# Up projection: the gate's sigmoid from exponentials and a logarithm on ScalarE, the weight low parts on VectorE

## The chip, the core and the metric

The program runs on one core of one Trainium2 chip. The metric is the device time of one execution in microseconds (us), the median of a few runs. A core has five engines that each work through a queue of their own: TensorE (PE; its weight loads are listed as PEld), VectorE (DVE), ScalarE (ACT), GpSimd (POOL) and SyncE (SP, which here only starts transfers). They wait for one another through semaphores.

## The reference, cut to what matters

The whole program is two blocks of a network on a 1024 x 1024 activation. The change touches one matrix product of the second block and the activation behind it:

```python
D_FF = 2816
def conv_ffn(h, w_up, conv_w, conv_b, w_down):
    T = h.shape[1]                       # 1024 positions
    u = h @ w_up                         # (1024 x 1024) @ (1024 x 5632)
    up = jnp.pad(u, ((0, 0), (CONV_W - 1, 0), (0, 0)))
    c = conv_b + sum(up[:, j:j + T] * conv_w[j] for j in range(CONV_W))   # 3 taps
    gate, val = jnp.split(c, 2, axis=-1)
    return (jax.nn.gelu(gate) * val) @ w_down
```

`jax.nn.gelu` is the tanh form, which is the same as gate * sigmoid(s * gate * (1 + 0.044715 gate^2)) with s = 2 sqrt(2/pi).

## The kernel before, in words

Every matrix product is done in three passes on rounded parts: a weight block W is split into a high part (ScalarE copies it to the rounded type, line 3469 in this phase, 401 in the others) and a low part (W minus the high part, line 3474 in this phase, 406 in the others); the activations are split likewise. TensorE adds up high x high, high x low and low x high.

The phase around the change is `up_part`. Its 2816 hidden columns are worked off in 22 groups j of 128 gate columns and the 128 value columns that belong to them. Of each group TensorE computes two units, ("up", j, 0), the gate, and ("up", j, 1), the value, each [128 columns x 1024 positions] in PSUM, in two pieces of 512 positions with 24 matmuls each (line 3541). A group is 96 matmuls. The units go round four PSUM banks.

The order on each queue is written out by hand; no scheduler moves anything. For one group:

- SyncE loads the weights of group j (line 3483) once unit ("up", j-2, 1) is done, since groups j and j-2 have the same slot of W.
- ScalarE, in iteration j: the high part of group j+1 (`up_w_hi`), the centre tap of the gate (line 3584), its square (3588), the exponential (3590), the centre tap of the value (3584).
- GpSimd: the low part of each group from 1 to 21 (`up_w_lo`), one after another. That of group 0 is made on VectorE, in the phase before.
- VectorE, in iteration j: the two other taps of the gate (3601, 3603; the second frees the PSUM bank), then the argument of the sigmoid (3614, 3615), 1 + the exponential (3617), the reciprocal (3618), the product with the gate (3619), the two taps of the value (3601, 3603) and the product of both (3624), which is written into `act_turned`.
- TensorE: groups 0 and 1 begin before all rows of the activation are there. It first does the left piece of all four units of groups 0 and 1. Behind the first and the second of these pieces it turns the last two row blocks (line 625) that the phase before (`out2`) has left over; then it does the four right pieces, and from group 2 on group after group. Before the left pieces of group 1, and before each later group, it waits for that group's low part (`K.up_lo`).

The phase before ends on VectorE with lines 602 and 616: value and low part of the turned rows; the last row block can only be finished when TensorE has turned it. The phase behind is `down`, the product with w_down. Its first weight block is split early (in iteration 21). Its second is loaded into a slot of W that unit ("up", 21, 1) frees, and split by lines 401 (ScalarE) and 406 (VectorE), followed by the low part of the activation (2571 on ScalarE, 2622 on VectorE). TensorE needs all of this for the second step of `down`. The third block goes where the gate's buffer is, so SyncE waits for `s_cg`, which VectorE gives after the last gate product.

Of the kernel before, what the change touches and what calls it, by code (L numbers as in the profile page):

```python
# [29 lines left out]
ALU = mybir.AluOpType  # L30
ACT = mybir.ActivationFunctionType
# [3426 lines left out]
def up_slots(K):  # L3458

    return [(K.pl.items[("down", 0, 0)] + n) % 3 for n in range(3)]  # L3460


def up_half(K, j, hi, W):
    return W[:, up_slots(K)[j % 2], HALF * hi:HALF * hi + HALF]


def up_w_hi(K, a, j):
    a.wait_ge(K.up_in[j % 2], 32 * (j // 2 + 1))
    a.activation(up_half(K, j, 1, K.Wr), up_half(K, j, 0, K.W), ACT.Copy).then_inc(K.up_hi, 1)


def up_w_lo(K, eng, j):
    eng.wait_ge(K.up_hi, j + 1)
    eng.tensor_tensor(up_half(K, j, 0, K.Wr), up_half(K, j, 0, K.W), up_half(K, j, 1, K.Wr).bitcast(F32), ALU.subtract)\  # L3474
        .then_inc(K.up_lo, 1)


def load_up(K, sp, j, done):

    dst = K.W[:, up_slots(K)[j % 2], 0:HALF].rearrange("p (k n) -> p k n", n=2 * P)  # L3480
    for half in range(2):
        c0 = FF * half + P * j
        sp.dma_start(dst[:, :, P * half:P * half + P],
                     K.i["w_up_2"][0][:, c0:c0 + P].rearrange("(k p) n -> p k n", p=P)).then_inc(done, 16)


def up_part(K, st, rows):

    nc = K.nc
    NJ = FF // P
    K.AT = nc.alloc_sbuf_tensor_at("act_turned", [P, NJ, T], F32, offset=K.base + 4 * 6 * T)
    K.ATr = nc.alloc_sbuf_tensor_at("act_turned_rounded", [P, NJ, T], F32R, offset=K.base + 4 * 6 * T)

    CUBE, SLOPE = 0.044715, 2 * math.sqrt(2 / math.pi)
    HL = K.uHL  # L3500
    slots = up_slots(K)
    cg = K.W[:, slots[2], 0:HALF].rearrange("p (a t) -> p a t", a=2)
    cv = K.W[:, slots[2], HALF:2 * HALF].rearrange("p (a t) -> p a t", a=2)
    G = K.ps(st, "G", [P, 4, T])
    first = K.pl.units[("up", 0, 0)]
    s_cg = K.sem("up_last_gate")
    s_c, s_sq, s_arg, s_e, s_at = (K.sem("up_centre"), K.sem("up_square"), K.sem("up_gelu_arg"),
                                   K.sem("up_gelu_exp"), K.sem("up_act_ready"))

    def bank(key):  # L3510
        return G[:, (K.pl.units[key] - first) % 4, :]

    def ht(k):
        return K.HTr[:, k, 0:T].rearrange("p (s n) -> p s n", n=C)

    def ht_lo(k):
        if k < 6:
            return HL[:, k, :].rearrange("p (s n) -> p s n", n=C)
        return K.HTr[:, 4 * (k - 6):4 * (k - 6) + 4, T:R]

    def sync(sp):
        for j in range(2, NJ):
            K.wait_unit(sp, ("up", j - 2, 1))
            load_up(K, sp, j, K.up_in[j % 2])
        for j in (NJ - 2, NJ - 1):
            K.wait_unit(sp, ("up", j, 1))
            K.load_item(sp)
        sp.wait_ge(s_cg, 1)

    def gpsimd(g):  # L3530
        for j in range(1, NJ):
            up_w_lo(K, g, j)

    def tensor(pe):
        def piece(j, half, rc):
            w = [up_half(K, j, n, K.Wr).rearrange("p (k n) -> p k n", n=2 * P) for n in range(2)]
            c = slice(P * half, P * half + P)
            for k in range(KT):
                x = [ht_lo(k), ht(k)]
                for a, b in SPLIT_PASSES:  # L3540
                    ins = pe.matmul(bank(("up", j, half))[:, rc * 512:rc * 512 + 512], w[a][:, k, c],  # L3541
                                    x[b][:, 2 * rc:2 * rc + 2, :], start=(k == 0 and a == b == 1),
                                    stop=(k == KT - 1 and a == 0))
            return ins

        early = [(j, half) for j in range(2) for half in range(2)]
        for n, (j, half) in enumerate(early):
            if half == 0:
                pe.wait_ge(K.up_lo, j + 1)
            if n == 0:  # L3550
                rows.taken(pe, rows.late[0] - 1)
                rows.ready(pe, 4)
            elif n < 3:
                rows.taken(pe, rows.late[n - 1])
            else:
                rows.turns_read(pe)
            piece(j, half, 0)
            if n < 2:
                rows.turn(pe, rows.late[n])
        rows.ready(pe, 8)  # L3560
        for j, half in early:
            piece(j, half, 1).then_inc(K.gemm_done, 1)
        for j in range(2, NJ):
            pe.wait_ge(K.up_lo, j + 1)
            for half in range(2):
                K.wait_bank(pe, ("up", j, half), 4)
                piece(j, half, 0)
                piece(j, half, 1).then_inc(K.gemm_done, 1)

    def scalar(a):  # L3570
        rows.done(a)
        for j in range(NJ):
            if 1 <= j and j + 1 < NJ:
                up_w_hi(K, a, j + 1)
            if j == NJ - 1:
                K.split_hi(a, ("down", 0, 0))
                K.early[0](a)
            for half, c in ((0, cg), (1, cv)):
                key = ("up", j, half)
                tile = j + NJ * half  # L3580
                K.wait_unit(a, key)
                if j >= 2:
                    a.wait_ge(s_at, j - 1)
                a.activation(c[:, j % 2, :], bank(key), ACT.Identity, scale=K.conv_w_col(2, tile),
                             bias=K.col("conv_b_2", tile)).then_inc(s_c, 1)
                if half == 0:
                    K.wait_read(a, key)
                    a.activation(K.AT[:, j, :], cg[:, j % 2, :], ACT.Square).then_inc(s_sq, 1)
                    a.wait_ge(s_arg, j + 1)
                    a.activation(K.AT[:, j, :], K.AT[:, j, :], ACT.Exp, scale=-SLOPE).then_inc(s_e, 1)  # L3590

    def vector(v):
        ch = Chain(v, K.v_chain, K.vn)
        rows.done(v)
        def conv(j, half, c):

            key = ("up", j, half)
            tile = j + NJ * half
            u = bank(key)
            v.wait_ge(s_c, 2 * j + half + 1)  # L3600
            ch.link(v.scalar_tensor_tensor(out=c[:, j % 2, 1:T], in0=u[:, 0:T - 1], scalar=K.conv_w_col(1, tile),
                                           in1=c[:, j % 2, 1:T], op0=ALU.mult, op1=ALU.add))
            K.free_bank(v.scalar_tensor_tensor(out=c[:, j % 2, 2:T], in0=u[:, 0:T - 2],
                                               scalar=K.conv_w_col(0, tile), in1=c[:, j % 2, 2:T],
                                               op0=ALU.mult, op1=ALU.add), key)

        for j in range(NJ):
            at, g = K.AT[:, j, :], cg[:, j % 2, :]
            if j == NJ - 1:
                K.split_lo(v, ("down", 0, 0))  # L3610
                K.early[1](v)
            conv(j, 0, cg)
            v.wait_ge(s_sq, j + 1)
            ch.link(v.tensor_scalar(at, at, CUBE, 1.0, ALU.mult, ALU.add))
            v.tensor_tensor(at, at, g, ALU.mult).then_inc(s_arg, 1)
            v.wait_ge(s_e, j + 1)
            ch.link(v.tensor_scalar(at, at, 1.0, None, ALU.add))
            ch.link(v.reciprocal(at, at))  # L3618
            ch.link(v.tensor_tensor(at, at, g, ALU.mult))
            if j == NJ - 1:  # L3620
                v.tensor_copy(K.zcol[:, 1:2], K.eps[:, :]).then_inc(s_cg, 1)
            conv(j, 1, cv)
            K.wait_read(v, ("up", j, 1))
            v.tensor_tensor(at, at, cv[:, j % 2, :], ALU.mult).then_inc(s_at, 1)
        K.vn = ch.n

    def done(eng):

        eng.wait_ge(s_at, NJ)

    def taken(pe, n):

        K.wait_read(pe, [("up", NJ - 2, 1), ("up", NJ - 1, 0), ("up", NJ - 2, 0)][n])

    def left(eng):

        K.wait_unit(eng, ("up", NJ - 1, 1))

    return Part(sync, gpsimd, tensor, scalar, vector, None, (), None, done, taken, left)


def phase_up(K):
# [184 lines left out]
def phase_gla_in(K):  # L3827
# [13 lines left out]
    with ExitStack() as st:  # L3841
        up = up_part(K, st, out2)
    with ExitStack() as st:
        down = down_part(K, st, up)
    with ExitStack() as st:
# [13 lines left out]
        @block.gpsimd  # L3859
        def _(g):  # L3860
            out1.gpsimd(g)
            diff.gpsimd(g)
            out2.gpsimd(g)
            up.gpsimd(g)
            down.gpsimd(g)
            ple.gpsimd(g)

# [64 lines left out]
```

## Time and profile before

| | |
|---|---|
| time before, median of 3 runs | 3481.53 us (3475.88 to 3481.85) |
| the profiled execution's own time | 3472.04 us |
| its span, first to last instruction | 3470.3 us |
| mean granted TensorE clock | 0.983 |
| PE busy | 3307.2 us (95%) |
| DVE busy | 1943.5 us (56%) |
| ACT busy | 1428.5 us (41%) |
| POOL busy | 197.7 us (6%) |
| TensorE's first and last matmul of the up projection start at | 2560.6 and 3056.5 us |

The profile is of one execution. Times in it count from the start of the span. Each engine's rows give the start, the duration and, in square brackets, how long the engine sat idle before and which instruction of which engine ended that. `act_turned<-act_turned,W` is read as: written tile, then the tiles read. G is the PSUM tile, W the weight buffer (in this phase its third slot also holds the two convolution results), W_rounded the same memory in the rounded type.

### The profile page before, as it was taken

What the parts mean: (1) busy time and instruction counts of PE and PEld (TensorE: products, weight loads), DVE (VectorE), ACT (ScalarE), POOL (GpSimd) and SP (SyncE); (2) the same over time, 40 slices, a digit from 0 to 9 for tenths busy, and PEclk for the clock granted to TensorE, in tenths of its full rate; (3) what the DMA queues carried; (4) which work ended last, traced back from release to release, by engine and by line L of the source; (5) the groups of instructions that cost most, each with busy time, mean ns of one, the idle gap of its engine ahead of it and who ended that gap; (6) DMA issues with size and microseconds to landing.
All of it is one profiled execution on the core that took longest, in us unless ns stands there. A gap on an engine that the chain in (4) does not pass through costs nothing. (4 is left out here: it accounts for less than half of the span.)

```text
span 3470.3 us, 42712 instructions
## 1 busy us (share of the span) xinstructions
PE 3307.2 (95%) x17536; PEld 2671.8 (77%) x17536; DVE 1943.5 (56%) x2754; ACT 1428.5 (41%) x2322; POOL 197.7 (6%) x245
## 2 busy tenths in 40 slices
PE   6999999999999999999998999988989999989997
PEld 5888888888777777787886777776777888878775
DVE  6554444444434466532885644348558888865544
ACT  5343434434233345125775434228433222234445
POOL 0000000000000000001000000000012122200000
PEclk9999999999999999999999999999999999999999
DMA  5202011111423565023201611010332111134453
GB/s 199 69 1 79 28 64 43 52 55 54 150 104 139 203 225 191 31 52 95 61 2 37 188 55 49 25 53 1 122 111 60 49 49 45 42 127 158 168 190 127
DMA packets 188532, 308.37 MB, mean 89 GB/s; under 512 B 28369, under 2 KB 122643, under 8 KB 188211
## 3 DMA queue, kind: packets, MB, share of 16 engines
q1 hardware_dynamic: 166275, 226.27, 20.3%
q0 software_dynamic: 19424, 74.14, 6.0%
q10 hardware_dynamic: 2640, 5.24, 0.4%
q8 instruction: 139, 2.28, 0.3%
q14 instruction: 54, 0.44, 0.0%
HBM read 269.87 MB, written 35.75 MB: 88 GB/s over the span
## 5 line engine op out<-in xcount | busy, mean ns | idle before, releaser
L406 DVE TENSOR_TENSOR W_rounded<-W,W_rounded 128x2048 fp32r<-128x2048 f32 x151 | 345.8, 2291 | 448.4 <-ACT W_rounded L401 445.3
L3541 PE MATMUL G<-HT_rounded,W_rounded 128*128 128x512 f32 x1584 | 452.4, 393 | 1.5 <-POOL W_rounded L3474 1.5
L401 ACT ACTIVATE W_rounded<-W 128x2048 fp32r<-128x2048 f32 x151 | 288.3, 1910 | 376.8 <-DMA W<-in_w_down 91.3
L3541 PEld LDWEIGHTS G<-HT_rounded,W_rounded 128*128 128x128 f32 x1584 | 297.9, 188 | 70.2 <-POOL W_rounded L3474 2.0
L2520 PE MATMUL G<-W_rounded,r_y_rounded 128*128 128x512 f32 x960 | 231.5, 402 | 11.4 <-DVE r_y_rounded L2622 9.7
L2520 PE MATMUL G<-W_rounded,x_hi 128*128 128x512 f32 x704 | 221.4, 396 | 12.7 <-DVE act_turned_rounded L2622 12.5
L2520 PEld LDWEIGHTS G<-W_rounded,r_y_rounded 128*128 128x128 f32 x960 | 182.0, 191 | 57.8 <-DVE W_rounded L406 10.8
L1139 PE MATMUL G<-W_rounded,HT_rounded 128*128 128x512 f32 x640 | 213.7, 415 | 0.0
L2177 PE MATMUL G<-HT_rounded,W_rounded 128*128 128x512 f32 (+1 forms) x768 | 208.0, 356 | 3.1 <-DVE W_rounded L406 3.1
L3541 PE MATMUL G<-HT_lo_ffn,W_rounded 128*128 128x512 f32 x528 | 208.3, 394 | 0.0
L1183 PE MATMUL G<-HT_rounded,W_rounded 128*128 128x512 f32 (+1 forms) x768 | 205.7, 354 | 1.0 <-PEq L643 1.0
L2836 PE MATMUL G<-W_rounded,HT_rounded 128*128 128x512 f32 x640 | 203.1, 399 | 0.0
L2520 PEld LDWEIGHTS G<-W_rounded,x_hi 128*128 128x128 f32 x704 | 132.5, 189 | 44.2 <-DVE W_rounded L406 13.7
L2177 PEld LDWEIGHTS G<-HT_rounded,W_rounded 128*128 128x128 f32 x768 | 136.6, 188 | 28.0 <-DVE W_rounded L406 4.0
L1183 PEld LDWEIGHTS G<-HT_rounded,W_rounded 128*128 128x128 f32 x768 | 136.0, 188 | 22.6 <-issue 1.2
L3618 DVE RECIPROCAL act_turned<-act_turned 128x1024 f32<-128x1024 f32 x22 | 144.2, 6553 | 0.8
L2836 PEld LDWEIGHTS G<-W_rounded,HT_rounded 128*128 128x128 f32 x640 | 118.4, 188 | 28.2 <-issue 2.0
L2520 PE MATMUL G<-W_rounded,act_turned_rounded 128*128 128x512 f32 x352 | 139.7, 397 | 0.0
L1139 PEld LDWEIGHTS G<-W_rounded,HT_rounded 128*128 128x128 f32 x640 | 120.2, 188 | 25.2
L1183 PE MATMUL G<-HT_lo,W_rounded 128*128 128x512 f32 (+1 forms) x384 | 136.4, 355 | 0.0
L2177 PE MATMUL G<-HT_lo,W_rounded 128*128 128x512 f32 (+1 forms) x384 | 136.4, 355 | 0.0
L1639 PE MATMUL G<-W_rounded,HT_rounded 128*128 128x512 f32 x416 | 132.4, 400 | 0.0
(462 smaller groups left out, 6655.3 us busy)
## 6 DMA issues: line engine op xcount, KB each, us to landing
W<-in_w_down SPq DMA_DIRECT2D x33, 1024.0 KB, 4.8
W<-in_ab_w_out SPq DMA_DIRECT2D x32, 1024.0 KB, 5.6
W<-in_w_up SPq DMA_DIRECT2D x44, 512.0 KB, 5.1
W<-in_ab_w_in SPq DMA_DIRECT2D x20, 1024.0 KB, 8.0
W<-in_w_mod SPq DMA_DIRECT2D x8, 2048.0 KB, 8.1
x_rows<-r_xt POOLq DMA_DIRECT2D x32, 512.0 KB, 5.3
W<-in_c_w_out SPq DMA_DIRECT2D x24, 512.0 KB, 6.8
r_xt<-x_rows POOLq DMA_DIRECT2D x24, 512.0 KB, 4.8
```

Source lines behind the costliest of these rows:

```text
L401: a.activation(self.half(key, True), self.half(key, False, False), ACT.Copy).then_inc(self.w_hi, 1)
L406: v.tensor_tensor(self.half(key, False), self.half(key, False, False), self.half(key, True).bitcast(F32), ALU.subtract).then_inc(self.w_lo, 1)
L1139: ins = pe.matmul(G[:, K.par(key), :], x[y][:, 4 * kh + k, r * P:(r + 1) * P], wv[z][:, k, :], start=(kh == 0 and k == 0 and (y, z) == SPL ...
L1183: ins = pe.matmul(G[:, K.par(key), 0:n], wv[y][:, k, cc], x[z][:, k, c0:c0 + n], start=(k == 0 and (y, z) == SPLIT_PASSES[0]), stop=(k == ...
L1639: ins = pe.matmul(bank(key), x[y][:, 4 * kh + k, r * P:(r + 1) * P], w[z][:, k, :], start=(kh == 0 and k == 0 and (y, z) == SPLIT_PASSES[0 ...
L2177: ins = pe.matmul(bank(key, n), w[y][:, k, cc], x[z][:, k, c0:c0 + n], start=(k == 0 and (y, z) == SPLIT_PASSES[0]), stop=(k == KT - 1 and ...
L2520: ins = pe.matmul(slot(r)[:, n * 512:(n + 1) * 512], x[y], w[z][:, k, n * 512:(n + 1) * 512], start=(kk == 0 and k == 0 and (y, z) == SPLI ...
L2836: ins = pe.matmul(bank(key), x[y][:, 4 * kh + k, r * P:(r + 1) * P], w[z][:, k, :], start=first, stop=last)
L3541: ins = pe.matmul(bank(("up", j, half))[:, rc * 512:rc * 512 + 512], w[a][:, k, c], x[b][:, 2 * rc:2 * rc + 2, :], start=(k == 0 and a == ...
L3618: ch.link(v.reciprocal(at, at))
```

## The change

For the gate of each group, sigmoid(x) was 1 / (1 + exp(-x)), with the exponential on ScalarE, and the sum and the reciprocal on VectorE. Now ScalarE makes it alone, in four instructions: Relu(x + 42), Exp(42 - that), Ln(1 + that), Exp(-that). The constant 0.044715 is put into the square on ScalarE, so that VectorE makes the argument with one instruction in place of two. The low parts of groups 1 to 21 move from GpSimd to VectorE: that of group 1 stands behind everything of the phase before, that of group j+1 (for j from 1 to 20) between the argument and the product of group j.

```diff
-    def gpsimd(g):
-        for j in range(1, NJ):
-            up_w_lo(K, g, j)
...
     def scalar(a):
+        ch = Chain(a, K.a_chain, K.an)
...
-                    a.activation(K.AT[:, j, :], cg[:, j % 2, :], ACT.Square).then_inc(s_sq, 1)
+                    at = K.AT[:, j, :]
+                    a.activation(at, cg[:, j % 2, :], ACT.Square, scale=math.sqrt(CUBE)).then_inc(s_sq, 1)
                     a.wait_ge(s_arg, j + 1)
-                    a.activation(K.AT[:, j, :], K.AT[:, j, :], ACT.Exp, scale=-SLOPE).then_inc(s_e, 1)
+                    ch.link(a.activation(at, at, ACT.Relu, scale=SLOPE, bias=K.cut[:, :]))
+                    ch.link(a.activation(at, at, ACT.Exp, scale=-1.0, bias=K.cut[:, :]))
+                    ch.link(a.activation(at, at, ACT.Ln, bias=K.one[:, :]))
+                    a.activation(at, at, ACT.Exp, scale=-1.0).then_inc(s_e, 1)
...
     def vector(v):
         ch = Chain(v, K.v_chain, K.vn)
+        up_w_lo(K, v, 1)
         rows.done(v)
...
             v.wait_ge(s_sq, j + 1)
-            ch.link(v.tensor_scalar(at, at, CUBE, 1.0, ALU.mult, ALU.add))
-            v.tensor_tensor(at, at, g, ALU.mult).then_inc(s_arg, 1)
+            v.scalar_tensor_tensor(out=at, in0=at, scalar=1.0, in1=g, op0=ALU.add, op1=ALU.mult).then_inc(s_arg, 1)
+            if 1 <= j and j + 1 < NJ:
+                up_w_lo(K, v, j + 1)
             v.wait_ge(s_e, j + 1)
-            ch.link(v.tensor_scalar(at, at, 1.0, None, ALU.add))
-            ch.link(v.reciprocal(at, at))
             ch.link(v.tensor_tensor(at, at, g, ALU.mult))
```

How the queues stand. VectorE at the start of the phase, behind the last rows of `out2` (line 616 is the low part of the last turned rows; W<-G are the convolution taps), before:

```order
L616 TENSOR_TENSOR HT_rounded<-row_room,HT_rounded 128x2x128
L3601 SCALAR_TENSOR_TENSOR W<-G,cols,W 128x1023
L3603 SCALAR_TENSOR_TENSOR W<-G,cols,W 128x1022
L3614 TENSOR_SCALAR act_turned<-act_turned 128x1024
L3615 TENSOR_TENSOR act_turned<-act_turned,W 128x1024
L3617 TENSOR_SCALAR act_turned<-act_turned 128x1024
L3618 RECIPROCAL act_turned<-act_turned 128x1024
L3619 TENSOR_TENSOR act_turned<-act_turned,W 128x1024
```

and VectorE at the same place now, through group 0 and to the low part of group 2 in iteration 1:

```order
L616 TENSOR_TENSOR HT_rounded<-row_room,HT_rounded 128x2x128
L3474 TENSOR_TENSOR W_rounded<-W,W_rounded 128x2048
L3605 SCALAR_TENSOR_TENSOR W<-G,cols,W 128x1023
L3607 SCALAR_TENSOR_TENSOR W<-G,cols,W 128x1022
L3618 SCALAR_TENSOR_TENSOR act_turned<-act_turned,W 128x1024
L3622 TENSOR_TENSOR act_turned<-act_turned,W 128x1024
L3605 SCALAR_TENSOR_TENSOR W<-G,cols,W 128x1023
L3607 SCALAR_TENSOR_TENSOR W<-G,cols,W 128x1022
L3627 TENSOR_TENSOR act_turned<-act_turned,W 128x1024
L3605 SCALAR_TENSOR_TENSOR W<-G,cols,W 128x1023
L3607 SCALAR_TENSOR_TENSOR W<-G,cols,W 128x1022
L3618 SCALAR_TENSOR_TENSOR act_turned<-act_turned,W 128x1024
L3474 TENSOR_TENSOR W_rounded<-W,W_rounded 128x2048
```

The first row L3474 is the low part of group 1, which stands behind line 616; the second is that of group 2, which stands behind all of group 0 and the gate's taps of group 1. Both were in GpSimd's queue, where nothing but the low parts stood between the transfers of `out2` and those of `down`.

VectorE at the end, from the last gate's taps to the second step of `down` (L406 is the low part of `down`'s second weight block, L2622 that of the activation), before:

```order
L3601 SCALAR_TENSOR_TENSOR W<-G,cols,W 128x1023
L3603 SCALAR_TENSOR_TENSOR W<-G,cols,W 128x1022
L3614 TENSOR_SCALAR act_turned<-act_turned 128x1024
L3615 TENSOR_TENSOR act_turned<-act_turned,W 128x1024
L3617 TENSOR_SCALAR act_turned<-act_turned 128x1024
L3618 RECIPROCAL act_turned<-act_turned 128x1024
L3619 TENSOR_TENSOR act_turned<-act_turned,W 128x1024
L3621 COPY zcol<-eps 128x1
L3601 SCALAR_TENSOR_TENSOR W<-G,cols,W 128x1023
L3603 SCALAR_TENSOR_TENSOR W<-G,cols,W 128x1022
L3624 TENSOR_TENSOR act_turned<-act_turned,W 128x1024
L406 TENSOR_TENSOR W_rounded<-W,W_rounded 128x2048
```

and VectorE at the same place now:

```order
L3605 SCALAR_TENSOR_TENSOR W<-G,cols,W 128x1023
L3607 SCALAR_TENSOR_TENSOR W<-G,cols,W 128x1022
L3618 SCALAR_TENSOR_TENSOR act_turned<-act_turned,W 128x1024
L3622 TENSOR_TENSOR act_turned<-act_turned,W 128x1024
L3624 COPY zcol<-eps 128x1
L3605 SCALAR_TENSOR_TENSOR W<-G,cols,W 128x1023
L3607 SCALAR_TENSOR_TENSOR W<-G,cols,W 128x1022
L3627 TENSOR_TENSOR act_turned<-act_turned,W 128x1024
L406 TENSOR_TENSOR W_rounded<-W,W_rounded 128x2048
L2622 TENSOR_TENSOR act_turned_rounded<-act_turned,x_hi 128x2x384
```

Three rows are gone ahead of L406 (an addition, a reciprocal and one of the two instructions of the argument), and no low part of the up projection stands here, since group 21 is the last.

## Rows read from the trace of the kernel before

**Rows 1.** Who PE waited for, 2550 to 3110 us: total, times, longest (us).

```profile
PE G L2520 <- DVE act_turned_rounded L2622: 9.4, 1, 9.4
PE TR L625 <- DVE r_xs L580: 3.2, 1, 3.2
PE G L3541 <- POOL W_rounded L3474: 1.5, 1, 1.5
```

**Rows 2.** PE busy by stretch: stretch, its us, busy us (count), granted clock, DMA share, GB/s.

```profile
2569.50:2573.70 4.20, 4.19 (x16) 0.59 0.35 138
2613.40:3056.60 443.20, 443.20 (x1920) 1.00 0.17 48
3074.50:3078.50 4.00, 3.96 (x10) 0.51 0.00 0
```

**Rows 3.** Groups by line, 2560 to 3075 us: count, busy us, mean ns, idle before.

```profile
L3618 DVE RECIPROCAL act_turned<-act_turned 128x1024 f32<-128x1024 f32 x22 | 144.2, 6553 | 0.8
...
L3474 POOL TENSOR_TENSOR W_rounded<-W,W_rounded 128x2048 fp32r<-128x2048 f32 x21 | 97.0, 4620 | 359.0 <-ACT W_rounded L3469 356.0 <-DMA x_rows<-r_xt 3.0
L3619 DVE TENSOR_TENSOR act_turned<-act_turned,W 128x1024 f32<-128x1024 f32 x22 | 76.9, 3498 | 0.8
...
L3617 DVE TENSOR_SCALAR act_turned<-act_turned 128x1024 f32<-128x1024 f32 x22 | 15.3, 695 | 24.8 <-ACT act_turned L3590 24.8
```

**Rows 4.** Timeline of PE, left piece of group 1: start, duration, instruction.

```profile
2578.39 0.47 PE L3541 MATMUL G<-HT_rounded,W_rounded 128*128 128x512 f32 x1
```

**Rows 5.** Timeline of DVE, end of `out2`: start, duration, instruction, [idle before].

```profile
2555.52 2.29 DVE L3474 TENSOR_TENSOR W_rounded<-W,W_rounded 128x2048 fp32r<-128x2048 f32 x1 [3.06 <-ACT W_rounded L3469]
...
2578.67 1.23 DVE L602 TENSOR_TENSOR row_room<-TR,cols 128x1024 f32<-128x1024 f32 x1 [1.03 <-PE TR L625]
...
2581.90 0.42 DVE L616 TENSOR_TENSOR HT_rounded<-row_room,HT_rounded 128x256 fp32r<-128x256 f32 x1
```

**Rows 6.** Timeline of ACT, group 0's gate and group 2's high part.

```profile
2595.34 1.21 ACT L3584 ACTIVATE W<-G,cols 128x1024 f32<-128x1024 f32 x1 [14.35 <-PE G L3541]
...
2606.76 1.92 ACT L3469 ACTIVATE W_rounded<-W 128x2048 fp32r<-128x2048 f32 x1 [2.21 <-DMA W<-in_w_up]
```

**Rows 7.** Timeline of DVE, group 0's gate.

```profile
2596.68 1.28 DVE L3601 SCALAR_TENSOR_TENSOR W<-G,cols,W 128x1023 f32<-128x1023 f32 x1 [14.36 <-ACT W L3584]
...
2600.41 0.69 DVE L3614 TENSOR_SCALAR act_turned<-act_turned 128x1024 f32<-128x1024 f32 x1 [1.13 <-ACT act_turned L3588]
```

**Rows 8.** Timeline of PE, first matmul of group 2.

```profile
2613.38 0.50 PE L3541 MATMUL G<-HT_rounded,W_rounded 128*128 128x512 f32 x1 [1.54 <-POOL W_rounded L3474]
```

**Rows 9.** Timeline of ACT in the last phase: Exp, then the last Exp of that chain.

```profile
3369.62 1.15 ACT L3788 ACTIVATE act_turned<-act_turned,cut 128x1024 f32<-128x1024 f32 x1
...
3371.99 1.06 ACT L3790 ACTIVATE act_turned<-act_turned 128x1024 f32<-128x1024 f32 x1
```

**Rows 10.** Timeline of DVE, group 20's product to the first instruction behind the group.

```profile
3043.93 1.22 DVE L3619 TENSOR_TENSOR act_turned<-act_turned,W 128x1024 f32<-128x1024 f32 x1
3045.18 1.28 DVE L3601 SCALAR_TENSOR_TENSOR W<-G,cols,W 128x1023 f32<-128x1023 f32 x1
...
3048.96 2.29 DVE L406 TENSOR_TENSOR W_rounded<-W,W_rounded 128x2048 fp32r<-128x2048 f32 x1
```

**Rows 11.** Timeline of ACT, group 21's gate and `down`'s second weight block.

```profile
3045.82 1.21 ACT L3584 ACTIVATE W<-G,cols 128x1024 f32<-128x1024 f32 x1 [3.55 <-PE G L3541]
...
3061.83 1.92 ACT L401 ACTIVATE W_rounded<-W 128x2048 fp32r<-128x2048 f32 x1 [1.94 <-DMA W<-in_w_down]
```

**Rows 12.** Timeline of DVE, `down`'s second step.

```profile
3071.25 2.28 DVE L406 TENSOR_TENSOR W_rounded<-W,W_rounded 128x2048 fp32r<-128x2048 f32 x1
3073.45 0.95 DVE L2622 TENSOR_TENSOR act_turned_rounded<-act_turned,x_hi 128x768 fp32r<-128x768 f32 x1
```

**Rows 13.** Timeline of PE: `down`'s second step, and another wait, in the last phase.

```profile
3074.55 1.19 PE L2520 MATMUL G<-W_rounded,x_hi 128*128 128x512 f32 x2 [9.45 <-DVE act_turned_rounded L2622]
...
3346.53 0.73 PE L3751 MATMUL G<-W_rounded,HT_rounded 128*128 128x512 f32 x2 [2.48 <-DVE W_rounded L406]
```

More of the change, by code:

```diff
@@ L3507, in up_part @@
     s_c, s_sq, s_arg, s_e, s_at = (K.sem("up_centre"), K.sem("up_square"), K.sem("up_gelu_arg"),
-                                   K.sem("up_gelu_exp"), K.sem("up_act_ready"))
+                                   K.sem("up_gelu_sigmoid"), K.sem("up_act_ready"))
     def bank(key):
@@ L3587, in scalar @@
                     K.wait_read(a, key)
-                    a.activation(K.AT[:, j, :], cg[:, j % 2, :], ACT.Square).then_inc(s_sq, 1)
+                    at = K.AT[:, j, :]
+                    a.activation(at, cg[:, j % 2, :], ACT.Square, scale=math.sqrt(CUBE)).then_inc(s_sq, 1)
                     a.wait_ge(s_arg, j + 1)
-                    a.activation(K.AT[:, j, :], K.AT[:, j, :], ACT.Exp, scale=-SLOPE).then_inc(s_e, 1)
+                    ch.link(a.activation(at, at, ACT.Relu, scale=SLOPE, bias=K.cut[:, :]))
+                    ch.link(a.activation(at, at, ACT.Exp, scale=-1.0, bias=K.cut[:, :]))
+                    ch.link(a.activation(at, at, ACT.Ln, bias=K.one[:, :]))
+                    a.activation(at, at, ACT.Exp, scale=-1.0).then_inc(s_e, 1)
+        K.an = ch.n
     def vector(v):
         ch = Chain(v, K.v_chain, K.vn)
+        up_w_lo(K, v, 1)
         rows.done(v)
@@ L3637, in left @@
         K.wait_unit(eng, ("up", NJ - 1, 1))
-    return Part(sync, gpsimd, tensor, scalar, vector, None, (), None, done, taken, left)
+    return Part(sync, None, tensor, scalar, vector, None, (), None, done, taken, left)
 def phase_up(K):
@@ L3863, in _ @@
             out2.gpsimd(g)
-            up.gpsimd(g)
             down.gpsimd(g)
```

## The prediction

> **What bounds the kernel now.** I first read the page (TensorE is busy for 95% of the span, VectorE for 56%), then, since the change lies in one phase, the busy time of that phase by stretches. From the first matmul of group 2 to the last of group 21 TensorE is busy in 443.2 of 443.2 us with the clock at 1.00, the upper of its two levels [rows 2]. Those are 20 groups of 96 matmuls, so a group takes 22.16 us and half a group (one unit) 11.08. In this stretch no engine makes TensorE wait, and whatever VectorE saves there buys nothing, although VectorE looks nearly full. Next I asked who TensorE waits for around the phase: 9.4 us at its end for VectorE, 1.5 for the low part of group 2, and 3.2 for a row block of the phase before, which the change doesn't touch [rows 1]. So the change can act in three places only: the low part of group 1, the low part of group 2, and the end. Then I laid the new queues over the timeline of each.
>
> **What goes and what comes, per group.** VectorE loses the reciprocal (6.55 us) and two instructions of 0.69 [rows 3, 7], and its product L3619 should fall from a mean of 3.50 to the 1.22 that it takes where GpSimd is still [rows 3, 10]. It gains a low part of 2.29 [rows 5]. ScalarE gets three instructions more; the like ones in the last phase follow each other in (3371.99 - 3369.62) / 2 = 1.19 us [rows 9]. The four thus take 3 x 1.18 + 1.06 = 4.6 us from the start of the first to the end of the last (at most 4.75, at least 4 x 1.06 = 4.24). All of it is hidden behind the 22.16 us of TensorE as long as the low part of the next group is ready when TensorE is.
>
> That holds in the steady groups. Counted from the end of the gate's unit, which has 11.08 us to go: ScalarE starts 0.3 later, the argument starts 5.07 after that (2600.41 - 2595.34) [rows 6, 7] and takes about 1.28, as the taps of nearly the same size [rows 10], and the low part 2.29. Sum 8.9, so 2.2 us are left. I take 0 for the 19 groups from 3 on.
>
> **Place 1, group 1.** TensorE wanted this low part at 2578.39 and had it [rows 4], since GpSimd made it beside the row work. Now it stands on VectorE behind the last row block, which has to be turned by TensorE first; its last instruction ends at 2581.90 + 0.42 = 2582.3 [rows 5]. With 2.29 for the low part it is ready at 2584.6, and TensorE stands for 6.2 us more. Nothing covers this, since group 1 is next in TensorE's queue and the right pieces stand behind it.
>
> **Place 2, group 2.** All in the time of before (the delay of place 1 shifts everything alike). The argument of group 0 starts at 2600.41 [rows 7], now ends at 2601.69; ScalarE's four end at 2601.72 + 4.6 = 2606.3; the product starts at 2606.35. From the product to the first instruction behind the group VectorE takes 3048.96 - 3043.93 = 5.03 [rows 10], so the taps of group 1 start at 2611.4; from there to the argument are 2600.41 - 2596.68 = 3.73 [rows 7], hence 2615.1; the argument 1.28, the low part 2.29: 2618.7. ScalarE's high part is earlier (data at 2606.76, done by about 2609.2 even behind the value tap [rows 6]). TensorE started at 2613.38 [rows 8] and now starts at 2618.75: +5.4 us.
>
> A rule on this place. GpSimd takes 4.62 us for a low part, VectorE 2.29 [rows 3, 5]. The Trainium skill ("GPSIMD Engine Reference", 3. Performance versus the Vector engine) says that elementwise work belongs on VectorE, which does such a subtraction in about half the time. The trace agrees on the duration. By this rule alone, low parts ready 2.3 us sooner, the wait of 1.54 us at group 2 would be gone; by the order of the queue it becomes 6.9.
>
> **The clock behind a wait.** After the 3.2 us wait and the 9.4 us one TensorE ran at the lower level (1.2 GHz) for a while: mean granted clock 0.59 over 4.2 us and 0.51 over 4.0 [rows 2]. That is a loss of 4.2 x 0.41 = 1.7 and 4.0 x 0.49 = 2.0 us; I take 1.8 each. After the wait of 1.54 us its matmuls were not slow, nor after one of 2.48: two matmuls in 0.73 us, against 1.19 behind the 9.45 us wait [rows 8, 13]. So places 1 and 2 (waits of 5.9 and 6.9 us in all) each cost another 1.8.
>
> **Place 3, the end.** The gate's centre tap of group 21 starts at 3045.82 [rows 11], the argument 5.07 later at 3050.89, the product 5.94 after that (2606.35 - 2600.41) at 3056.83. The value's centre tap can start 11.08 after the gate's, at 3056.90, and VectorE's tap 1.34 later (2596.68 - 2595.34) [rows 6, 7], so VectorE is through with the group about 3.8 us on, at 3062.0. Before it was at 3071.25 [rows 12]. What is late next is the weight block of `down`: its data come at 3061.83, its high part is done at 3063.75 [rows 11]. Then L406, L2622 2.20 after it (3073.45 - 3071.25), TensorE 1.10 after that (3074.55 - 3073.45) [rows 12, 13]: 3067.1. That is 7.4 us less of the wait, and the 2.0 us that remain are shorter than the 2.48 after which the clock stayed up, so another 1.8 come back: -9.2.
>
> A rule on what gets faster here. L3619 took 3.50 us in the mean and 1.22 where no low part ran on GpSimd [rows 3, 10]. The Trainium skill ("SBUF — State Buffer", Who interferes with whom) says that a VectorE instruction with two inputs in SBUF and a GpSimd instruction that reads SBUF exclude each other for the whole of the instruction. By it L3619 is short everywhere once GpSimd has no arithmetic; if instead 3.50 were its own, place 2 would be 2.3 us later still.
>
> **The sum.** 6.2 + 1.8 + 5.4 + 1.8 - 9.2 = +6.0 us. Against the profiled execution's own 3472.04 that is 3478.0. The median of the runs is 3481.53, 9.5 above that execution; on it the forecast is 3487.5. Bounds: ScalarE's four (4.24 to 4.75) move place 2 by -0.4 to +0.2; each clock loss lies between 1.7 and 2.0; if the clock falls at the end all the same, +1.8. So +5 to +8.
>
> **Rivals.**
>
> *The end gains less, since two transfers meet.* SyncE may load `down`'s third block once the last gate product is done, at about 3058.2 instead of 3067.5. The second block, in flight from 3056.6 to 3061.8, then shares the DMA engines with it. If they share evenly, the 3.5 us left of it take 7, TensorE resumes at 3070.6 after a wait of 5.5, and the clock falls: 6.0 + 3.5 + 1.8 = +11.3, slower, 3493. It decides as soon as the second block lands over 0.5 us late (then the wait passes 2.48). For: equal sizes, started 1.6 us apart. Against: one queue issues both, in order.
>
> *The low part comes late in every group.* If the chain from the gate's unit to the low part takes over 11.08 us instead of 8.9, each of 19 groups pays the excess: 1 us too much is +19, 3507, slower. It decides from 2.2 us on. Against: each term is read from a row; for: ScalarE, once idle in this phase, now has work of its own between.
>
> *Only the low part's speed counts.* If the low parts weren't kept back by what stands before them, the 1.5 us of group 2 go and the end gains 9.2: -10.7, 3471, faster. Against: the order of VectorE's queue is plain, and the last rows wait for TensorE's own turn.
>
> *The activation doesn't do what it says:* VectorE's time falls, but the pace of the groups was VectorE's, so they get shorter. Against: no idle of TensorE in 443 us, so at most 0. I give it no chance of its own.
>
> **Chances.** Forecast 0.70, meeting transfers 0.15, late low parts 0.06, speed alone 0.09. What a measurement of this kernel can tell from no change is about 0.2%, 7 us; the runs before spread over 6. The forecast lies just inside that, so of its 0.70 I give 0.50 to "within" and 0.20 to "slower". Slower: 0.20 + 0.15 + 0.06 = 0.41; faster 0.09; same 0.50. The range goes from 3477 (the forecast on a fast set of runs) to 3497 (the meeting transfers with some more).
>
> **What would show it.** Right: TensorE waits for VectorE's L3474 twice, some 5.9 and 6.9 us, the second at the start of group 2, each followed by about 4 us at the lower clock; no other wait for L3474, and busy throughout from group 2 on; L3622 at 1.2 us; the wait in front of `down`'s second step about 2 us with the weight's transfer as the last cause. VectorE's busy time in the phase falls by more than 150 us. Wrong: a short wait at groups 1 or 2, a wait at each group, or a wait of over 5 us at `down`.

## The result and the profile after

The changed kernel takes 3483.68 us, the median of 20 runs (3481.05 to 3490.18); the kernel before takes 3477.82, the median of 20 (3471.46 to 3485.93). The ratio is 1.0019, with a 95% interval of 1.0013 to 1.0025: 5.9 us more by the medians, about where the forecast of +6.0 was. The profiled execution took 3482.47 us, 10.4 more than that of before.

VectorE did what the change says: its busy time over the phase is 261.1 us (from 2560 to 3085 us) in place of 438.6 (from 2560 to 3075), which is 177 us less. None of it reached the time by itself. What did are three waits of TensorE, with its clock behind them. First who TensorE waited for around the phase (us in total, times, longest), the view of [rows 1]:

```profile
PE G L3537 <- DVE W_rounded L3474: 12.6, 2, 6.7
PE TR L625 <- DVE r_xs L580: 3.2, 1, 3.2
PE G L2520 <- DVE act_turned_rounded L2622: 1.9, 1, 1.9
PE TR L625 <- DVE row_room L602: 1.3, 1, 1.3
```

The reader is to see that 9.4 us of waiting at `down` have become 1.9, and that 1.5 at the low part of group 2 have become 12.6 at two low parts, 5.9 at group 1 and 6.7 at group 2. The waits for `r_xs` and `row_room` belong to the phase before and are those of before; the second of them was 1.4 us there, a row that [rows 1] doesn't show. Next the timeline of TensorE at the three places (start, duration, instruction, what ended its idle time), which answers to [rows 4, 8, 13]:

```profile
2587.99 0.80 PE L3537 MATMUL G<-HT_rounded,W_rounded 128*128 128x512 f32 x1 [5.93 <-DVE W_rounded L3474]
...
2629.67 0.79 PE L3537 MATMUL G<-HT_rounded,W_rounded 128*128 128x512 f32 x1 [6.71 <-DVE W_rounded L3474]
...
3086.01 1.07 PE L2520 MATMUL G<-W_rounded,x_hi 128*128 128x512 f32 x2 [1.94 <-DVE act_turned_rounded L2622]
```

and VectorE at the same three places: the last row block and the low part of group 1, then the low part of group 2, then the weight block of `down` (answering to [rows 5, 7, 12]):

```profile
2582.10 1.23 DVE L602 TENSOR_TENSOR row_room<-TR,cols 128x1024 f32<-128x1024 f32 x1 [4.03 <-PE TR L625]
...
2585.32 0.42 DVE L616 TENSOR_TENSOR HT_rounded<-row_room,HT_rounded 128x256 fp32r<-128x256 f32 x1
2585.66 2.28 DVE L3474 TENSOR_TENSOR W_rounded<-W,W_rounded 128x2048 fp32r<-128x2048 f32 x1
...
2617.43 1.22 DVE L3622 TENSOR_TENSOR act_turned<-act_turned,W 128x1024 f32<-128x1024 f32 x1 [4.68 <-ACT act_turned L3591]
...
2627.33 2.28 DVE L3474 TENSOR_TENSOR W_rounded<-W,W_rounded 128x2048 fp32r<-128x2048 f32 x1
...
3082.71 2.29 DVE L406 TENSOR_TENSOR W_rounded<-W,W_rounded 128x2048 fp32r<-128x2048 f32 x1 [1.74 <-ACT W_rounded L401]
```

Each low part ends when TensorE starts (2585.66 + 2.28 = 2587.94, TensorE at 2587.99; 2629.61 and 2629.67). Ahead of the first, VectorE had sat idle for 4.03 us with the high part long ready, since its next instruction in order was the row block that TensorE still had to turn. Ahead of the second stands group 0. At the end VectorE is through early and waits for ScalarE's high part.

The busy time of TensorE by stretches, the view of [rows 2], shows what follows the waits:

```profile
2587.90:2592.10 4.20, 4.11 (x11) 0.61 0.00 0
2629.60:2636.00 6.40, 6.33 (x16) 0.53 0.00 0
2657.00:3075.40 418.40, 418.40 (x1814) 1.00 0.17 48
3086.00:3090.20 4.20, 4.19 (x12) 0.59 0.73 289
```

Groups 3 to 21 run without a gap, as before. After each of the three waits the granted clock (fifth number) is at the lower level for a while, after the third one too. The losses (length of the stretch times what the clock lacked) are 4.2 x 0.39 = 1.6 us, 6.4 x 0.47 = 3.0 and 4.2 x 0.41 = 1.7.

With that the difference inside the phase adds up. From the restart behind the wait for `r_xs` to the start of `down`'s second step it is 505.04 us before (2569.51 to 3074.55) and 513.04 after (2572.97 to 3086.01), 8.0 us more. The waits give 5.9 + 6.7 + 1.9 - 1.5 - 9.4 = +3.6, the clock behind the first two 1.6 + 3.0 = +4.6, together 8.2. Behind `down`'s second step the clock cost 1.7 in place of 2.0, so the three places account for +7.9. The other 2.5 of the 10.4 us lie where the change touches nothing. Ahead of the phase the kernel after is 3.5 us later (2572.97 against 2569.51), 2.7 of them by the step that starts at 2532.12 before and at 2534.85 after; the clock behind that step's wait, 0.73 over 6.4 us before and 0.59 after, makes up the rest. From `down`'s second step to the end it is 1.1 us shorter (394.7 against 395.8); the clock behind a wait in the last phase fell before (0.68 over 4.2 us) and not after.

### The profile page after: what moved, and what is told of

Read it like the earlier page. It is cut to its first block and busy times, and to the rows that moved or that the text cites. A ratio compares the mean times of both kernels' runs of the same rounds, so it can differ in the third digit from the quotient of the medians.

```text
span 3480.7 us, 42710 instructions
## 1 busy us (share of the span) xinstructions
PE 3312.5 (95%) x17536; PEld 2675.3 (77%) x17536; DVE 1763.2 (51%) x2709; ACT 1506.9 (43%) x2388; POOL 100.6 (3%) x224
## 3 DMA queue, kind: packets, MB, share of 16 engines
q8 instruction: 139, 2.28, 0.3%
## 5 line engine op out<-in xcount | busy, mean ns | idle before, releaser
L406 DVE TENSOR_TENSOR W_rounded<-W,W_rounded 128x2048 fp32r<-128x2048 f32 x151 | 345.7, 2290 | 457.9 <-ACT W_rounded L401 454.5
L3537 PE MATMUL G<-HT_rounded,W_rounded 128*128 128x512 f32 x1584 | 455.9, 395 | 12.6 <-DVE W_rounded L3474 12.6
L401 ACT ACTIVATE W_rounded<-W 128x2048 fp32r<-128x2048 f32 x151 | 288.3, 1910 | 383.2 <-DMA W<-in_w_down 92.6
L3605 DVE SCALAR_TENSOR_TENSOR W<-G,cols,W 128x1023 f32<-128x1023 f32 x44 | 56.4, 1283 | 164.2 <-ACT W L3581 164.1
```

The lines of the kernel that those rows point to most:

```text
L401: a.activation(self.half(key, True), self.half(key, False, False), ACT.Copy).then_inc(self.w_hi, 1)
L406: v.tensor_tensor(self.half(key, False), self.half(key, False, False), self.half(key, True).bitcast(F32), ALU.subtract).then_inc(self.w_lo, 1)
```

## The experiments

All times are medians of 4 to 11 runs beside 20 to 22 of the kernel before on the same chip; ratios are to that one, with their 95% intervals. The edits are against the changed kernel unless it is said otherwise, and cut (...) to what matters; a function `gpsimd` of `up_part` is called in GpSimd's queue between `out2` and `down`, as before. The theory: the time follows from where three instructions stand in VectorE's queue. The rivals: it follows from VectorE's load, from GpSimd's contention with it, or from the speed of a low part.

**1. The low part of group 1 back on GpSimd.**

```diff
+    def gpsimd(g):
+        for j in (1,):
+            up_w_lo(K, g, j)
...
-        up_w_lo(K, v, 1)
         rows.done(v)
```

VectorE also waits for GpSimd's low part ahead of its own first one, in this kernel and the next, so that the count of finished low parts stays in order; in neither trace does it ever stand for it.

> The changed kernel, but the low part of group 1 is made on GpSimd again; those of groups 2 to 21 stay on VectorE. Theory (what costs is where the low parts of groups 1 and 2 stand in VectorE's queue): TensorE's wait of 5.9 us ahead of group 1 goes, with the 1.6 us lost to the lower clock behind it; the wait of 6.7 at group 2 and the one of 1.9 at the end stay. About 7.5 us less than the changed kernel, which was 5.9 above before: 1.6 us below before. Rival (the time follows VectorE's total work or GpSimd's contention with it): one low part of 22 moved changes nothing, +5.9 stays or grows.

Measured: 3475.56 us, ratio 0.9995 (0.9986 to 1.0003), where the changed kernel has 1.0019. TensorE's waits around the phase, without the one for `row_room` (0.9 us):

```profile
PE G L3541 <- DVE W_rounded L3474: 6.7, 1, 6.7
PE TR L625 <- DVE r_xs L580: 3.2, 1, 3.2
PE G L2520 <- DVE act_turned_rounded L2622: 2.0, 1, 2.0
```

One instruction of 2.3 us, moved back to the slower engine, gives 0.0024 of the time back, some 8 us: the wait of 5.9 and the clock behind it. VectorE's load differs by this one instruction, out of 261 us. The rival of the load falls here.

**2. The low parts of groups 1 and 2 back on GpSimd.**

```diff
+        for j in (1, 2):
+            up_w_lo(K, g, j)
...
-            if 1 <= j and j + 1 < NJ:
+            if 2 <= j and j + 1 < NJ:
```

> The changed kernel, but the low parts of groups 1 and 2 are made on GpSimd again, 3 to 21 stay on VectorE. Theory: no wait at group 1; at group 2 the high part is ready 0.5 us later than before (ScalarE has the sigmoid first) and GpSimd needs 4.6, so a wait of 2.0 instead of 1.5 and of 6.7. Together with the end (wait 1.9 instead of 9.4) 7 to 9 us below before, 9 if the clock stays up behind the wait of 2.0 us. Rival (VectorE's load): as the changed kernel.

Measured: 3470.07 us, ratio 0.9976 (0.9967 to 0.9984), 7.8 us below before. TensorE's wait at group 2 is 2.05 us, as expected; behind it the clock fell (0.60 over the next 4.2 us), where it had stayed up behind the 1.54 us of before; the result lies in the lower half of the gain that was expected. The other 19 low parts are on VectorE here.

**3. The sigmoid alone: all low parts on GpSimd.**

```diff
-        up_w_lo(K, v, 1)
         rows.done(v)
...
-            if 1 <= j and j + 1 < NJ:
-                up_w_lo(K, v, j + 1)
```

> Only the first half of the change: the sigmoid on ScalarE and the shorter argument, all low parts on GpSimd as before. Theory: the steady groups don't mind where the low parts are made, so the same as with groups 1 and 2 on GpSimd alone: 7 to 9 us below before. VectorE's instructions with two inputs in SBUF are stretched again where they meet a low part, and it costs nothing. Rival (removing the contention is what pays): slower than that by several us, up to 19 groups times 2.3.

Measured: 3469.73 us, ratio 0.9970 (0.9958 to 0.9982). It can't be told from the one before it, although 19 more low parts are on GpSimd; the wait at group 2 is 2.05 us again, with the clock at 0.61 behind it. Contention is there and moved to another instruction, the last product of a group (L3628 here), as the groups by line show (count, busy us, mean ns, idle before):

```profile
L3628 DVE TENSOR_TENSOR act_turned<-act_turned,W 128x1024 f32<-128x1024 f32 x22 | 37.5, 1705 | 0.8
L3623 DVE TENSOR_TENSOR act_turned<-act_turned,W 128x1024 f32<-128x1024 f32 x22 | 27.0, 1225 | 102.9 <-ACT act_turned L3595 102.9
...
L3474 POOL TENSOR_TENSOR W_rounded<-W,W_rounded 128x2048 fp32r<-128x2048 f32 x21 | 97.0, 4620 | 360.9 <-ACT W_rounded L3469 358.1 <-DMA x_rows<-r_xt 2.8
```

L3628 takes 1.71 us in the mean against 1.22, and the time doesn't notice: what contention costs once the reciprocal is gone is less than these runs can tell.

**4. The low parts alone: the reciprocal stays.** Against the kernel before, and without its low parts on GpSimd:

```diff
+        up_w_lo(K, v, 1)
         rows.done(v)
...
             v.tensor_tensor(at, at, g, ALU.mult).then_inc(s_arg, 1)
+            if 1 <= j and j + 1 < NJ:
+                up_w_lo(K, v, j + 1)
```

> Only the second half of the change: the low parts on VectorE at the same places, the sigmoid with exponential and reciprocal as before. Theory: group 1 costs the same, 5.9 + 1.6; at group 2 the reciprocal of group 0 (6.55 us) now stands ahead of the low part, which comes about 28.7 us after the end of group 0's gate instead of 23.4, so a wait of about 12 us (before: 1.5) and about 2.3 of clock; the steady groups still hold (9.6 of 11.08 us); the end keeps its wait of 9.4. Sum about +20 us on before. So the halves aren't additive: -8 and +20 against +6 together. Rival (the halves add up): -8 and +14.

Measured: 3493.64 us, ratio 1.0044 (1.0031 to 1.0056), so +15 and not +20. The waits of the phase:

```profile
PE G L3537 <- DVE W_rounded L3474: 17.9, 2, 11.9
PE G L2520 <- DVE act_turned_rounded L2622: 5.5, 1, 5.5
```

Groups 1 and 2 wait 5.9 and 11.9 us, as expected. The end doesn't wait 9.4, as I had written, but 5.5. Where the 3.9 come from is seen on VectorE at the gate of group 21. Before:

```profile
3051.16 0.95 DVE L2540 TENSOR_TENSOR act_turned_rounded<-act_turned,x_hi 128x768 fp32r<-128x768 f32 x1
3052.03 1.28 DVE L3601 SCALAR_TENSOR_TENSOR W<-G,cols,W 128x1023 f32<-128x1023 f32 x1
```

and with the low parts on VectorE and the reciprocal kept:

```profile
3074.74 0.95 DVE L2540 TENSOR_TENSOR act_turned_rounded<-act_turned,x_hi 128x768 fp32r<-128x768 f32 x1
3075.61 1.28 DVE L3598 SCALAR_TENSOR_TENSOR W<-G,cols,W 128x1023 f32<-128x1023 f32 x1
```

ScalarE had the centre tap ready at 3045.82 + 1.21 = 3047.0 before [rows 11], so VectorE came 5.0 us late to it, with a backlog. Here ScalarE's ends at 3074.53 (start 3073.32), and VectorE is 1.1 late. So before, the end was late by VectorE's backlog as well as by the reciprocal, and either half of the change works that off (with the sigmoid alone VectorE takes this tap 0.03 us behind ScalarE, at 3053.43). With the low parts alone its work is not less: the product with the gate (L3619 before) falls from 76.9 us to 27.0, and the low parts bring 48. But they fill the time in which VectorE stood waiting for the exponential, 24.8 us over the 22 groups before [rows 3] and 2.3 here (L3616). The halves don't add up (-8 and +15 against +6 together). By the waits: at group 2 the low parts alone wait 11.9 us and both together 6.7, since the reciprocal of group 0 no longer stands ahead; at the end they share a gain.

**5. Both low parts on VectorE, at other places.**

```diff
                 for r in due(s, 3):
                     B.vec_lo(v, r)
+            if s == len(steps) + 3 and tail is not None:
+                tail[2](v, 1)
...
-            if 1 <= j and j + 1 < NJ:
+            if 2 <= j and j + 1 < NJ:
                 up_w_lo(K, v, j + 1)
...
             conv(j, 1, cv)
+            if j == 0:
+                up_w_lo(K, v, 2)
```

> The changed kernel with two low parts in other places of VectorE's queue: that of group 1 ahead of the last row block, where VectorE sits idle for 4.0 us, that of group 2 already in group 0, between the taps of the value and its product. Theory: no wait at group 1; at group 2 the low part ends 17.4 us after the gate of group 0 where TensorE wants it at 16.8, a wait of about 0.7 (before 1.5); the end as in the changed kernel (wait 1.9, lower clock behind it or not). 8.5 to 10 us below before, 14 to 16 below the changed kernel. Rival (low parts on VectorE cost by their number): near the changed kernel.

Measured: 3466.88 us, ratio 0.9973 (0.9964 to 0.9982), 10.0 us below before and about 16 below the changed kernel. It has the same instructions on the same engines as the changed kernel; only the places of two differ. VectorE between the last two row blocks:

```profile
2577.54 0.42 DVE L616 TENSOR_TENSOR HT_rounded<-row_room,HT_rounded 128x256 fp32r<-128x256 f32 x1
2577.88 2.29 DVE L3476 TENSOR_TENSOR W_rounded<-W,W_rounded 128x2048 fp32r<-128x2048 f32 x1
2581.44 1.23 DVE L602 TENSOR_TENSOR row_room<-TR,cols 128x1024 f32<-128x1024 f32 x1 [1.28 <-PE TR L625]
```

and TensorE's waits:

```profile
PE G L2520 <- DVE act_turned_rounded L2624: 1.9, 1, 1.9
...
PE G L3539 <- DVE W_rounded L3476: 1.0, 2, 0.6
```

The low part of group 1 now fills idle time, and TensorE still makes VectorE wait behind it. Group 2 waits 0.6 us. A second wait of 0.5, at group 3, is new; probably, since with group 2 on time VectorE has less of a lead there, which was not tested.

**6. The same, and the activation split ahead of the weight block in `down`'s second step.**

```diff
-                if steps[s] not in presplit:
+                if steps[s] not in presplit and not (raw is not None and s == 1):
                     K.split_hi(a, steps[s])
...
                     a.activation(y_part(s, 1), y_part(s, 0, False), ACT.Copy).then_inc(s_yhi, 1)
+                if raw is not None and s == 1:
+                    K.split_hi(a, steps[s])
```

(the same exchange for `split_lo` on VectorE)

> As the one before, and in the second step of the down projection ScalarE and VectorE split the activation first and the weight block behind it, since the weight block is what comes last. Theory: TensorE's wait at the end falls from 1.9 to about 1.0 us; if the clock falls behind a wait of 1.9 and not behind 1.0, another 1.6. 0.9 to 2.6 us below the kernel before it. Rival: the step is bound by something else than the block's arrival, no difference.

Measured: 3466.09 us, ratio 0.9969 (0.9958 to 0.9980). The wait is 0.9 us in place of 1.9, as expected; the time could not be told from 5. Both once more, side by side on another chip:

> The kernel placed once more, to set it against placed_swap on one chip: 0.9973 of before again, within 0.001. Its profile shows a wait of 1.9 us ahead of the second step of the down projection; behind it the clock falls or stays, as in the seven executions so far (three fell, four stayed).

> placed_swap once more. Theory: 1.0 us less for the shorter wait and, since behind a wait of 1.9 us the clock fell in three of seven profiles with a loss of 1.6 each, on average 0.7 more: 1 to 3 us below placed. Rival: no difference (within 0.5 us).

Measured: 0.9974 (0.9965 to 0.9983; 3466.35 us) and 0.9973 (0.9964 to 0.9982; 3465.87 us). The waits are 2.1 us (the clock stayed up behind it) and 1.1. The second kernel is 0.5 to 0.8 us below the first both times. That is the sign of the theory and far less than the intervals, some 3 us to either side, can resolve. It stays open.

**7. How much room the steady groups have.** One and three instructions of 1.25 us ahead of the argument in groups 3 to 20:

```diff
+            if 3 <= j <= 20:
+                for _ in range(1):                    # 3 in the other kernel
+                    ch.link(v.tensor_tensor(at, at, at, ALU.max))
             v.scalar_tensor_tensor(out=at, in0=at, scalar=1.0, in1=g, ...
```

> The changed kernel with one more VectorE instruction of 1.25 us (the maximum of a tile with itself, in place) ahead of the argument in groups 3 to 20. Theory: the low part of the next group is ready 2.5 us before TensorE wants it, so this costs nothing: as the changed kernel, 5.9 above before. Rival (low parts are already late in every group, or near it): up to 18 x 1.25 = 22 us more.

> The same with three such instructions, 3.76 us. Theory: now each of 18 groups is late by 3.76 - 2.5 = 1.25 us, 22 us more than the changed kernel and 28 above before, TensorE waiting 18 times for a low part on VectorE; if the clock stays up behind such short waits. Rival (slack far larger than read, since the chain starts earlier than taken): no difference; (clock falls each time): 22 + 18 x 1.6 = 51 us more.

Measured: one, 3483.59 us, ratio 1.0019 (1.0010 to 1.0028), the changed kernel's own; three, 3510.34 us, ratio 1.0098 (1.0084 to 1.0112), which is 26.8 us more than with one. With three, TensorE waits at every one of the 18 groups (two of them in time order):

```profile
2677.98 0.50 PE L3537 MATMUL G<-HT_rounded,W_rounded 128*128 128x512 f32 x1 [1.19 <-DVE W_rounded L3474]
...
2701.60 0.50 PE L3537 MATMUL G<-HT_rounded,W_rounded 128*128 128x512 f32 x1 [1.19 <-DVE W_rounded L3474]
```

The room is thus about 2.5 us, more than one such instruction and less than three. A group now takes 2701.60 - 2677.98 = 23.62 us in place of 22.16: 1.46 more for a wait of 1.19. A wait costs some 0.27 us beyond its idle time. In part that is how idle time is counted: a matmul of 0.39 us is followed by the next after 0.23 us, and idle time starts only at its end. 18 x 1.46 = 26.3 of the 26.8. I had expected 22. The clock stayed up behind all 18.

## Why the prediction was right

**What bounds the kernel**: right. 177 us of VectorE's work gone and TensorE without a gap from group 3 on; experiment 1, where moving a single low part moves the time by 8 us, shows that place counts and load doesn't.

**Place 1**: forecast a delay of 6.2 us and a wait of 5.9, measured 6.1 (group 1 starts 15.02 us behind the restart at 2572.97 in place of 8.88) and 5.93. Experiments 1 and 5 remove it in two ways.

**Place 2**: forecast 6.9, measured 6.71. The argument took 1.23 and not 1.28, and what follows starts a little before it ends. Experiment 2 removes most of it.

**Place 3**: forecast a wait of 2.0 left, measured 1.94, and the weight block the last to come, as the row with [1.74 <-ACT W_rounded L401] shows. What I left out is why VectorE was late there before; experiment 4 shows 3.9 of the 9.4 us to have been backlog.

**The clock** was the term that was mis-sized, and one reading under it was false. Forecast: +1.8 and +1.8 at places 1 and 2, and 1.8 back at the end. In the profiled execution: 1.6, 3.0, and nearly nothing back (0.3), since the clock fell behind the 1.94 us too. The prediction took a wait of 2.48 us as one after which the clock stayed up, from the two matmuls directly behind it [rows 13]. It did not stay up; it fell some 1.5 us later. The same place over its first microsecond and over 4.2 us, and another wait of that profile, of 1.98 us:

```profile
3346.50:3347.50 1.00, 0.97 (x4) 1.00 1.02 406
3346.50:3350.70 4.20, 4.17 (x13) 0.68 0.45 178
...
3326.60:3330.80 4.20, 4.20 (x12) 0.61 1.08 361
```

So the row that the prediction leans on does not bear the 1.8 us back. The profile of before has both: 0.61 behind this wait of 1.98 us, 1.00 behind one of 2.00 us (at 1290.47). A fall at the end needed a chance of its own, and not only a place in the upper bound. At the end of the phase eight profiles have a wait of 1.9 to 2.1 us, and behind it the clock fell in three and stayed in five. The profiled waits and clock, +7.9, are 1.9 above the sum, and the sum of the waits alone, +3.6, is below its 6.2 + 5.4 - 7.4 = +4.2. That the medians differ by 5.9, on the forecast to 0.1 us, is in part luck: the interval of the ratio means 4.5 to 8.7 us, and with one profile of each kernel the runs don't say how often the clock fell at each place in the others. What is shown is the waits, and the sign.

**The steady groups**: forecast 2.2 us of room, measured about 2.5, cost 0.

**The rivals.** Meeting transfers: `down`'s second block was asked for when unit (21, 1) ended and its high part started 4.9 us later, in both kernels. The third block took a delay: asked for at about 3077.0, split from 3087.41, which is 10.4 us where it was 5.1 (3067.5 to 3072.56). The wait at the end stayed at 1.94, so this rival falls. Why the third block took longer is another matter. The prediction left out three transfers of 0.5 MB that GpSimd asks for right behind the phase, `r_xt<-x_rows`, at 3057.15 before and here:

```profile
3076.38 1.58 POOL L518 DMA_DIRECT2D r_xt<-x_rows  x3 [504.03 <-PE G L3537]
```

Before, they had 10 us until the third block was asked for; after, 0.7. From 3080.80 to 3087.40 the core moved 417 GB/s, 2.8 MB, more than twice the third block. So its delay fits these transfers at least as well as a turn behind the second block, and no run separates the two. ScalarE's two high parts after (start, duration, instruction, idle before; the first answers to the second row of [rows 11]):

```profile
3080.76 1.92 ACT L401 ACTIVATE W_rounded<-W 128x2048 fp32r<-128x2048 f32 x1 [3.68 <-DMA W<-in_w_down]
...
3087.41 1.91 ACT L401 ACTIVATE W_rounded<-W 128x2048 fp32r<-128x2048 f32 x1 [4.00 <-DMA W<-in_w_down]
```

Late low parts: only with three more instructions in the chain. Speed alone: the lower price of a low part on VectorE was real (2.29 against 4.62) and bought nothing at either place. Experiment 5 shows what it gives where the order lets it: about the gain that this rival forecast (10.7 below; measured 10.0) came about by moving two instructions.

**Two rules against the trace.** That elementwise work belongs on VectorE (the Trainium skill, "GPSIMD Engine Reference", 3. Performance versus the Vector engine) would have made the kernel faster by the durations; the queue's order decided. That the two engines exclude each other (the Trainium skill, "SBUF — State Buffer", Who interferes with whom) fits the trace: the product with the gate (L3619 before) took 1.22 us in the mean in every kernel without low parts on GpSimd, also with the reciprocal kept (experiment 4), and 3.50 before. One of before ran from 3021.69 to 3026.00, and the low part beside it on GpSimd ended at 3024.92, so that its own 1.2 us lie nearly all behind. The saving lay off the path, apart from the backlog at the end.

## What to carry to other kernels

Before moving work to a faster engine, ask what stands ahead of it in that engine's queue at the first and the last use, not in the steady loop: here two of 21 moved instructions cost more than all the rest gained, and with these two further ahead in the same queue the kernel is faster than either version. An engine that is idle while it waits for its next instruction in order is where such work goes. Split a change into its halves before judging it: -8 and +15 made +6, and only the waits showed why. And read the clock behind a wait over several microseconds, not from the first two matmuls.

## What was not expected of the hardware

- Behind a wait of about 2 us TensorE's clock may fall to its lower level (1.2 GHz) or not, in the same place of nearly the same program. The stretch of 4.2 us from the end of the wait at `down`'s second step, in experiment 1 (wait 2.02 us; the fifth number is the clock, the one in brackets the count of matmuls):

```profile
3073.10:3077.30 4.20, 4.14 (x18) 1.00 0.74 293
```

  The same stretch with one more instruction per group (wait 1.92 us):

```profile
3090.80:3095.00 4.20, 4.17 (x18) 1.00 0.73 291
```

  And with three more (wait 1.91 us):

```profile
3111.90:3116.10 4.20, 4.15 (x11) 0.59 0.74 294
```

  In the kernel after it is the row 3086.00:3090.20 above, 0.59 and 12 matmuls. Two waits of the last phase say the same over all twelve profiles: behind the one of 2.46 to 2.49 us the clock fell in nine and stayed up in three, and behind the one of 1.8 to 2.4 us ahead of it it fell in eleven. The shortest of these is in the kernel after, 1.80 us:

```profile
3337.60:3341.80 4.20, 4.15 (x12) 0.63 1.08 370
```

  Behind 18 waits of 1.19 it never fell. Longer waits are no sure thing either: the wait of 3.1 to 3.2 us for `r_xs` was followed by a fall in eleven profiles, and in the second one of experiment 6 by none (1.00 over 4.2 us behind 3.14).
- At the places of this study a fall cost between 1.5 and 3.0 us, and the larger figures come from stretches of up to 6 us at the lower level. A single figure of 1.8 was too narrow.
- A wait of 1.19 us lengthens a group by 1.46.
- Two transfers of 1 MB asked for 1.2 us apart on one queue, with three of 0.5 MB from GpSimd's queue asked for between them: the first wasn't slowed (4.9 us to the split of its data in both kernels), the last took 10.4 in place of 5.1.
